# One decoder layer with 32 experts on one core: expert biases added by single fp32r matmuls, and expert weights read in runs of 16 KB

## What is computed

```python
t = rmsnorm(x, norm_moe).reshape(256, 1024)
top_v, top_i = lax.top_k(t @ w_router + b_router, 4)       # 4 of 32 experts for a token
combine = ...                                              # softmax of top_v, spread to (256, 32)
for w1, b1, w2, b2, ce in experts:                         # w1 (1024, 2048), w2 (1024, 1024)
    u = t @ w1 + b1
    g, lin = min(u[:, :1024], 7), clip(u[:, 1024:], -7, 7)
    y = (g * sigmoid(1.702 * g) * (lin + 1)) @ w2 + b2
    acc += ce[:, None] * y
```

## Time and profile before

| | |
|---|---|
| median of 3 runs | 1445.66 us (1444.25 to 1447.10) |
| profiled execution | 1445.8 us, the same as its span, first to last instruction |
| PE busy | 1379.8 us (95%) |
| DVE busy | 469.5 us (32%) |
| ACT busy | 343.7 us (24%) |
| HBM read | 473.0 MB |

### The profile page before, as it was taken

One profiled execution on the slowest core, in us unless ns is written; L12 is line 12 of the kernel. 1 busy time (PEld: TensorE's weight loads), 2 busy tenths in 40 slices (PEclk: granted clock), 3 DMA queues, 4 the chain that ended last, 5 costly groups with the idle time before them and its releaser, 6 DMA issues.

```text
span 1445.8 us, 18689 instructions
## 1 busy us (share of the span) xinstructions
PE 1379.8 (95%) x7799; PEld 758.1 (52%) x7799; DVE 469.5 (32%) x796; ACT 343.7 (24%) x494; POOL 10.2 (1%) x27
## 2 busy tenths in 40 slices
PE   6999999999998999999999999999999999999996
PEld 6999988999997333333333333333333333333332
DVE  4653554444565222212122122121221212212222
ACT  5454544564343110101101011010110101101102
POOL 1000000000000000000000000000000000000000
PEclk9999999999998899999999999999999999999998
DMA  9453533536459799999999999999899999999993
GB/s 297 150 191 127 175 121 126 221 117 251 175 207 369 289 409 410 409 410 410 410 410 410 410 410 410 409 410 410 344 411 410 410 410 410 410 410 410 409 410 141
DMA packets 141273, 474.68 MB, mean 328 GB/s; under 512 B 8112, under 2 KB 10224, under 8 KB 141200
## 3 DMA queue, kind: packets, MB, share of 16 engines
q1 hardware_dynamic: 139776, 473.01, 83.7%
q10 hardware_dynamic: 1456, 1.07, 0.3%
HBM read 473.02 MB, written 1.05 MB: 328 GB/s over the span
## 4 chain that ended last, share of the span: by engine, by line
PE 89%; DVE 6%; ACT 3%; issue 1%; DMA 0%; SPq 0%; DVEq 0%; ACTq 0%
PE bank L1330 52%; PE bank L1168 26%; PE bank L1398 4%; DVE big_a L1060 2%; DVE big_a L1064 2%; DVE big_a L1057 2%; PE bank L1383 1%; ACT fxqT L731 1%; ACT p_a L734 1%; PE bank L1331 1%; PE bank L1178 1%; DMA ring<-in_w_in 0%; PE bank L1270 0%; PE bank L1289 0%; PE bank L1246 0%
## 5 line engine op out<-in xcount | busy, mean ns | idle before, releaser
L1330 PE MATMUL bank<-place,fxqT 128*64 128x512 f32 x1536 | 678.0, 594 | 24.4 <-ACT fxqT L731 24.4
L1331 PE MATMUL bank<-place,fxqT 128*64 128x512 f32 x1536 | 678.2, 595 | 0.0
L1330 PEld LDWEIGHTS bank<-place,fxqT 128*64 128x64 f32 x1536 | 208.2, 137 | 452.0 <-issue 452.0
L1331 PEld LDWEIGHTS bank<-place,fxqT 128*64 128x64 f32 x1536 | 208.4, 137 | 0.0
L788 DVE TENSOR_TENSOR w_lo<-ring,w_hi 128x2048 fp32r<-128x2048 f32 x64 | 146.7, 2292 | 161.3 <-ACT w_hi L510 161.2
L510 ACT ACTIVATE w_hi<-ring 128x2048 fp32r<-128x2048 f32 x64 | 122.6, 1916 | 173.5 <-PE bank L1168 170.8
L1168 PE MATMUL bank<-h_hi,w_hi 128*128 128x256 f32 x448 | 130.1, 290 | 2.5 <-DVE h_lo L778 2.5
L1168 PE MATMUL bank<-h_lo,w_hi 128*128 128x256 f32 x448 | 128.4, 287 | 0.0
L1168 PE MATMUL bank<-h_hi,w_lo 128*128 128x256 f32 x448 | 128.3, 286 | 0.0
L1047 DVE TENSOR_TENSOR fxqT<-bank,cols 128x256 f32<-128x256 f32 x66 | 24.9, 419 | 265.3 <-PE bank L1343 265.3
L1057 DVE TENSOR_SCALAR big_a<-bank 128x512 f32<-128x512 f32 x32 | 22.1, 691 | 252.6 <-PE bank L1331 252.6
(11 more groups left out here) (255 smaller groups left out, 1737.6 us busy)
## 6 DMA issues: line engine op xcount, KB each, us to landing
place<-in_w_exp_in SPq DMA_DIRECT2D x128, 2048.0 KB, 19.2
place<-in_w_exp_out SPq DMA_DIRECT2D x64, 2048.0 KB, 15.1
ring<-in_w_in SPq DMA_DIRECT2D x19, 2048.0 KB, 7.8
ring<-in_w_branch SPq DMA_DIRECT2D x6, 2048.0 KB, 8.1
ring<-in_w_mem_kv SPq DMA_DIRECT2D x4, 2048.0 KB, 8.1
ring<-in_w_out SPq DMA_DIRECT2D x2, 2048.0 KB, 11.7
ring<-in_w_in SPq DMA_DIRECT2D x2, 1024.0 KB, 8.4
xs<-in_x SPq DMA_DIRECT2D x2, 512.0 KB, 4.2
```

The source lines that it names most:

```text
L1330: mm(o[0:CAP, :], lhsT, low, start=start, stop=stop)
L1331: return mm(o[CAP:P, :], lhsT, high, start=start, stop=stop)
```

## The change

1. A transfer of expert weights is laid out so that partition p holds four rows next to each other, 4p to 4p + 3 of its block of 512. For w2 that is one run of 16 KB. For w1, whose rows are 8 KB (gate and linear part), a transfer now takes two whole rows of each partition, again one run of 16 KB; a transfer then holds both parts, so PE goes over the four transfers with gate and linear part inside, and both accumulate until the fourth. The operands follow this order of rows: ScalarE writes `got` through a view that reads PSUM in steps of 4 floats, VectorE writes `act_out` in steps of 128 floats, and the gain comes from a new small tile `g_rows`.
2. The biases are split in a rounded part and what is left of it, both fp32r, stacked in four groups of 32 partitions (both column halves), and `pick_e` becomes a [128, 2, 64] fp32r operand that holds a one in four rows. One matmul with 128 output columns replaces a pair: two for b1 (at the start), one for b2.
3. To prepare that: four DMAs each for b1 and b2 on ScalarE's queue in place of one, b1's at slot 60 behind a wait for `o_split`, a rounding copy on ScalarE at slots 50 and 62 (each behind a wait for the DMAs), subtractions on GpSimd in place of the two clears, the table `row_of` on GpSimd, and `g_rows` by a DMA of 16-byte pieces at slot 0.
4. VectorE's gate step waits for `gate_done`, given after the last gate matmul of the fourth transfer, where it waited for the second transfer.

```diff
-                part_, low = j // 2, D // 2 * (j % 2)
-                src = w[:, low:low + D // 2, FF * part_:FF * (part_ + 1)].rearrange("e (k p) n -> p (e k) n", p=P)
-                sp.dma_start(w1_buf[p][j][:, :, :], src).then_inc(w1_in[p][j], 16)
+                half, q = j // 2, 2 * (j % 2)
+                src = w[:, D // 2 * half:D // 2 * (half + 1), :].rearrange("e (p q) n -> p (e q n)", q=4)
+                sp.dma_start(w1_buf[p][j][:, :, :].rearrange("p k n -> p (k n)"),
+                             src[:, 2 * FF * q:2 * FF * (q + 2)]).then_inc(w1_in[p][j], 16)
...
-                src = w[:, FF // 2 * j:FF // 2 * (j + 1), :].rearrange("e (k p) n -> p (e k) n", p=P)
+                src = w[:, FF // 2 * j:FF // 2 * (j + 1), :].rearrange("e (p q) n -> p (e q n)", q=4)
...
-            pool.memset(b2rows[:, :], 0.0).then_inc(b2_zero, 1)
...
-            pool.memset(b1rows, 0.0).then_inc(b1_zero, 1)
+            pool.memset(row_of[:, :, :], 0.0).then_inc(row_step, 1)
...
+            def what_is_left(raw, split, left):
+                for n, r in enumerate((32, 96)):
+                    pool.tensor_tensor(split[r:r + 32, :], raw[r:r + 32, :], split[r:r + 32, :].bitcast(F32),
+                                       ALU.subtract).then_inc(left, 1)
...
+                    act.dma_start(g_rows[:, :, :],
+                                  norm_moe[0].rearrange("(h p q) -> p h q", h=2, q=4)).then_inc(router_in, 16)
...
+                if i == 50:
+                    act.wait_ge(b2_in, 64)
+                    act.activation(b2split[:, :], b2raw[:, :], ACT.Copy).then_inc(b2_rounded, 1)
+                if i == 60:
+                    act.wait_ge(o_split, 6)
+                    for r in range(4):
+                        half = b_exp_in[0].rearrange("e (q h n) -> e q h n", q=2, h=2)[:, :, r // 2, :]
+                        act.dma_start(b1raw[32 * r:32 * r + 32, :].rearrange("e (q n) -> e q n", q=2),
+                                      half).then_inc(b1_in, 16)
                 if i == 62:
-                    act.wait_ge(b1_zero, 1)
-                    act.dma_start(b1rows[0:NE, :], b_exp_in[0]).then_inc(b1_in, 16)
+                    act.wait_ge(b1_in, 64)
+                    act.activation(b1split[:, :], b1raw[:, :], ACT.Copy).then_inc(b1_rounded, 1)
...
-                act.activation(got, bank[2][:, :], ACT.Copy).then_inc(got_ready, 1)
+                act.activation(got.rearrange("c (q p) -> c q p", q=4), bank[2][:, :].rearrange("c (p q) -> c q p", q=4),
+                               ACT.Copy).then_inc(got_ready, 1)
...
-                dve.wait_ge(w1_used[p][1], mg + 1)
+                dve.wait_ge(gate_done, n + 1)
...
-                dve.tensor_tensor(act_out, lin, sig, ALU.mult).then_inc(act_ready, 1)
+                dve.tensor_tensor(act_out.rearrange("c (q p) -> c p q", q=4), lin.rearrange("c (p q) -> c p q", q=4),
+                                  sig.rearrange("c (p q) -> c p q", q=4), ALU.mult).then_inc(act_ready, 1)
...
                 for part_ in range(2):
-                    o, c = bank[part_], FF * part_
-                    both_halves(o, pick_e[:, :], b1rows[:, c:c + 512], b1rows[:, c + 512:c + FF], True, False)
...
+                    mm(bank[part_][:, :], pick_all, b1split[:, 512 * part_:512 * (part_ + 1)], start=True, stop=False)
+                for j in range(W1):
+                    half = j // 2
+                    pe.wait_ge(w1_in[p][j], mg * 16 + 16)
+                    rows_ = w1_buf[p][j][:, :, :].rearrange("p (q a) n -> p q (a n)", q=2)
+                    for part_ in range(2):
+                        c = FF * part_
+                        for i in range(2):
+                            w = rows_[:, i, c:c + FF]
+                            ins = both_halves(bank[part_], gotT[:, 2 * (j % 2) + i, half, :], w[:, 0:512], w[:, 512:FF],
+                                              False, j == W1 - 1 and i == 1)
+                        if j == W1 - 1 and part_ == 0:
+                            ins.then_inc(gate_done, 1)
+                    ins.then_inc(w1_used[p][j], 1)
+                    if j == 1:
                         pe.wait_ge(put_added, n * 4 + 4)
-                        both_halves(bank[5], pick_e[:, :], b2rows[:, 0:512], b2rows[:, 512:D], True, False)
+                        mm(bank[5][:, :], pick_all, b2split[:, :], start=True, stop=False)
```

More of the change, by code:

```diff
@@ L144, in build @@
         gsig = big_a[:, 0:2 * D].rearrange("p (c s) -> p c s", c=KT)
-        merged = sb("merged", [P, KT, S])
-        qkT, kmT = merged, merged
-        b1rows = merged[:, :, :].rearrange("p c s -> p (c s)")
+        with nc.sbuf_tensor("merged", [P, KT, S], F32) as merged:
+            qkT, kmT = merged, merged
+        b1raw = sb("b1raw", [P, D])
+        b1split = sb("b1split", [P, D], F32R)
+        final_dump = big_a[:, 0:2 * D].rearrange("p (t d) -> p t d", t=TT)
         gfin = sb("gfin", [P, D])
@@ L165, in build @@
         wr = sb("wr", [P, KT, NE])
+        g_rows = sb("g_rows", [P, 2, 4])
         br = sb("br", [P, NE])
@@ L174, in build @@
         p_a = sb("p_a", [P, 512])
-        p_bt = sb("p_bt", [P, 1024])
-        p_b, p_t = p_bt[:, 0:512], p_bt[:, 512:1024]
-        b2rows = p_bt
+        with nc.sbuf_tensor("p_bt", [P, 1024], F32) as p_bt:
+            p_b, p_t = p_bt[:, 0:512], p_bt[:, 512:1024]
+        b2raw = sb("b2raw", [P, 512])
+        b2split = sb("b2split", [P, 512], F32R)
         negmax = sb("negmax", [P, 2])
@@ L198, in build @@
         yS = p_a[:, :]
-        pick_e = sb("pick_e", [P, CAP])
+        row_of = sb("row_of", [P, 2, NE + 1])
+        pick_e = sb("pick_e", [P, 2, CAP], F32R)
         sel = sb("sel", [P, TT, CAP])
@@ L293, in build @@
         sq_ready, rstd_ready = sem("sq_ready"), sem("rstd_ready")
-        b1_zero, b2_zero, round_end = sem("b1_zero"), sem("b2_zero"), sem("round_end")
+        round_end = sem("round_end")
+        row_step, row_of_ready = sem("row_step"), sem("row_of_ready")
+        b1_rounded, b1_left, b2_rounded, b2_left = (sem(n) for n in ("b1_rounded", "b1_left", "b2_rounded", "b2_left"))
         selT_done, selWT_ready = sem("selT_done"), sem("selWT_ready")
-        gate_ready, sig_ready, ffn_step, aT_ready = (sem(n) for n in ("gate_ready", "sig_ready", "ffn_step", "aT_ready"))
+        gate_done, gate_ready, sig_ready, ffn_step, aT_ready = (sem(n) for n in ("gate_done", "gate_ready", "sig_ready", "ffn_step", "aT_ready"))
         yS_ready, put_done, put_added = (sem(n) for n in ("yS_ready", "put_done", "put_added"))
@@ L460, in _ @@
                                        channel_multiplier=-1).then_inc(ml_masked, 1)
-            pool.wait_ge(proj_done, FIRST["g1"] + 1)
-            pool.memset(b2rows[:, :], 0.0).then_inc(b2_zero, 1)
-            pool.wait_ge(o_split, 6)
-            pool.memset(b1rows, 0.0).then_inc(b1_zero, 1)
+            pool.memset(row_of[:, :, :], 0.0).then_inc(row_step, 1)
+            pool.wait_ge(row_step, 1)
+            for half in range(2):
+                pool.affine_select(out=row_of[:, half, 0:NE], in_=row_of[:, half, 0:NE], compare_op=ALU.not_equal,
+                                   fill=1.0, base=-64 * half, pattern=[[-1, NE]],
+                                   channel_multiplier=1).then_inc(row_step, 1)
+            pool.wait_ge(row_step, 3)
+            for half in range(2):
+                pool.affine_select(out=row_of[:, half, 0:NE], in_=row_of[:, half, 0:NE], compare_op=ALU.not_equal,
+                                   fill=1.0, base=-64 * half - 32, pattern=[[-1, NE]],
+                                   channel_multiplier=1).then_inc(row_of_ready, 1)
+            def what_is_left(raw, split, left):
+                for n, r in enumerate((32, 96)):
+                    pool.tensor_tensor(split[r:r + 32, :], raw[r:r + 32, :], split[r:r + 32, :].bitcast(F32),
+                                       ALU.subtract).then_inc(left, 1)
+                    pool.wait_ge(left, n + 1)
+            pool.wait_ge(row_of_ready, 2)
+            pool.wait_ge(b2_rounded, 1)
+            what_is_left(b2raw, b2split, b2_left)
+            pool.wait_ge(b1_rounded, 1)
+            what_is_left(b1raw, b1split, b1_left)
         ALL_CONSTS = 9
@@ L1039, in pick_expert @@
             def pick_expert(e):
-                dve.tensor_copy(pick_e[:, :], ident[:, bass.ds(e, 1)].to_broadcast([P, CAP])).then_inc(pick_ready, 1)
+                dve.tensor_copy(pick_e[:, :, :],
+                                row_of[:, :, bass.ds(e, 1)].to_broadcast([P, 2, CAP])).then_inc(pick_ready, 1)
             def take_turned(k):
                 dve.wait_ge(got_turned, k)
-                weights = g_moe.rearrange("p (h q) -> p q h", h=2)
+                weights = g_rows[:, :, :].rearrange("p h q -> p q h")
                 for h in range(2):
@@ L1094, in experts @@
                 dve.sem_inc(round_end, 1)
+            dve.wait_ge(row_of_ready, 2)
             dve.sem_inc(put_added, 4)
```

(5 more changed lines are left out.)

22 lines of the change are left out of this document (7 added, 15 removed).

## The result

| | before | changed |
|---|---|---|
| median | 1445.1 us (1444.3 to 1447.1, 4 runs) | 1415.1 us (1412.8 to 1415.8, 4 runs) |
| ratio | | 0.9784 (95%: 0.9770 to 0.9798) |
| profiled execution: span, time | 1445.8, 1445.8 us | 1411.0, 1412.8 us |
| TensorE's period, an expert | 29.98 us | 29.01 us |
| read rate in the expert stage | 410 GB/s | 428 GB/s |

The kernel became 2.2% faster. The forecast was 1403 us; the measured time lies 12 us above it, inside the range of 1388 to 1430.

The account below looks back on a forecast made before the run. TensorE was taken to set the pace with DMA close behind. 1445.8 us less 42.9 (32 experts at 28.64 us each), less 0.4 for the first expert's clock, plus 0.5 for preparation gave 1403.0 us; range 1388 to 1430.

Parts of the forecast that it names:

- windows of 410 to 420 GB/s, set by PE: Sign expected in the expert stage: read rate of 410 to 420 GB/s, with TensorE setting it.
- runs of 16 KB: Expert weight loads: 2 MB in 4.85 us in place of 5.115, from a fixed 11.8 ns a run.
- B: Expert loads: long runs gain less than the two rates say, 1406 us at half the step, 1419 at a quarter; chance 0.11.
- C: Expert loads: long runs do nothing, 410 GB/s stays and DMA binds, span 1432 us; chance 0.11.
- D: Expert loads: DMA gets worse as engines collide in memory, slower than before from 5.19 us a load; chance 0.04.
- the strided write: VectorE's act_out step in each expert, written in jumps of 512 bytes: 0.36 us more, bounds 0 and 0.7.
- Rival A: Expert stage: strides cost nothing, 28.28 us an expert, 1391.5 us; inside the forecast's range, which had chance 0.66.
- That `got` costs nothing: ScalarE's read of PSUM in steps of 16 bytes: no cost to TensorE even at double length, at most 0.2 us.
- the changes of array shape: The b2 matmul between pairs of 64 columns: going to the full array and back adds 0.15 us an expert.
- nothing is added there: Expert's start: L1398 was taken as full-array beside the full-array b1 matmul, so no shape cost, 0 us.
- E: New bias matmuls at 0.43 us and shape changes at 0.4: 0.82 us more an expert, 1429 us; chance 0.07.
- the hole at the change of order: Read gap where w2(19) waits for TensorE to leave w2(18): shrinks from 4.3 us to 1.3 us.

Follow-up runs that it names:

- The bias half alone: Changed kernel with weights back in four runs of 4 KB and got and act_out in order, split biases kept: 1438.5 us, ratio 0.9946 against the kernel before.
- The 8 KB experiment: Changed kernel with each w1 transfer in two runs of 8 KB a partition, w2 still at 16 KB: 1416.0 us, ratio 0.9780 against the kernel before.

## Why the prediction was right or wrong

**Right: what bounds.** TensorE sets the pace before and after, and DMA stands close behind. The bias half alone shows it best: without quicker loads it gives 8 us. One sign I gave was wrong by my own sum: I expected windows of 410 to 420 GB/s, set by PE. At 29.1 us of loads an expert against a period of 28.64, loads are always queued and the window shows DMA's own rate, as it did (428).

**Right: runs of 16 KB.** 428 GB/s, where two rates gave 434 and I took 432. A 2 MB load takes 2097152 / 428e3 = 4.90 us and a run (eight to an engine) 612.5 ns, so with the 159.8 ns of 4 KB the fixed part is (4 x 159.8 - 612.5) / 3 = 8.9 ns a run, not 11.8. The 8 KB experiment agrees with this size. By it runs of 2 KB would go at 389 GB/s; the window of the earlier trace rows that had 382 held other work too, which may be why, and no run shows it. Rivals B, C and D fall. The Trainium skill (DMA: Bandwidth & Descriptors, "Why small descriptors are slow") would have had 417 GB/s; the measurement decides.

**Right: the strided write.** 0.36 us was taken from a reduction read in jumps, 1.05 - 0.69 = 0.36 was measured. Rival A falls. That the two agree so closely is luck: the one is a read in jumps of 128 bytes, the other a write in jumps of 512. That `got` costs nothing held too, but for a better reason than mine: it does not get longer at all.

**Wrong in size: the changes of array shape.** The step "That is 0.15 us; bounds 0 and 0.4", and "nothing is added there" for b1. Against 0.24 a matmul plus 0.15, b2 measured 0.57 (0.18 more) and the two b1 0.67 (0.19 more). Together 0.37 us an expert: 28.64 + 0.37 = 29.01, the whole error of the period, 11.8 us in 32 experts. The price of the way back, 0.05, came from 705.18 in the earlier trace rows, where TensorE had just waited 0.76 us for ScalarE, so that whatever else it costs lay in the wait. Between busy matmuls a visit to the full array costs 0.2 more; the runs show this price once a visit, and not how the way in and the way back share it. The Trainium skill (TensorEngine Tiling (Array Packing), "Key Properties") says that changing the tiling mode drains TensorE; it has no figure, and the runs show what it costs here: 0.2 us a visit between busy matmuls and, as far as can be seen, none of it in a wait. At the expert's start I had taken L1398 for a full-array matmul with nothing added behind it. Its matmuls use 64 rows, a shape of their own, and leaving it costs the same towards either shape. Before, then in the changed kernel, the last four records of L1398 and what follows:

```profile
713.99 1.05 PE L1398 MATMUL bank<-p_a,fxqT 64*128 64x512 f32 x4
714.97 0.64 PE L1330 MATMUL bank<-merged,pick_e 128*64 128x512 f32 x1
```

```profile
703.06 1.05 PE L1446 MATMUL bank<-p_a,fxqT 64*128 64x512 f32 x4
704.05 0.51 PE L1403 MATMUL bank<-b1split,pick_e 128*128 128x512 f32 x1
```

0.98 and 0.99 us. So leaving the 64 rows costs what it did, the visit to the full array behind it is new, and I had left it out.

**Which rival this is.** The chance was highest for 1388 to 1410, and the time missed that. It lies where B had put it (1406 to 1420), but by luck: B's cause, slower loads, did not come. It is half of E, for which I had worked out 1416: of its two parts the fp32r matmuls cost no more than forecast and the changes of shape 0.37 us. I had given E 0.07.

**From the forecast to the measured time.** 1403.0 + 11.8 = 1414.8, against 1415.1 for the median. The profiled execution is 2.4 below its median. Its first expert started at full granted clock (half clock, 1.2 GHz, ended at 469 us, before it ended at 478), against 0.68 in the earlier trace rows:

```profile
470.00:482.00 12.00, 10.68 (x49) 3.88 (x51) 0.99 (x4) 1.70 (x2) 0.00 (x0) 1.00 0.43 165
```

Its mean granted clock is 0.989, that of the other three executions 0.986; that these ran at half clock for longer at this place is likely but not shown: the profiled execution of the kernel before has 0.989 too, with half clock up to 478. From the first bias record to the end of w2 of the last expert the two traces differ by 33.7 us: 32 x 0.975 = 31.2, and 2.6 for the 5.1 us that before ran at half clock.

**Wrong, without effect: the hole at the change of order.** I had 1.3 us, on the idea that a smaller lead shrinks it. Windows of the changed kernel over the hole, after it and at the end of the loads, and SyncE's queue:

```profile
1008.00:1018.00 10.00, 8.72 (x44) 3.04 (x42) 3.67 (x9) 2.10 (x4) 0.00 (x0) 1.00 0.00 0
1050.00:1380.00 330.00, 313.51 (x1423) 109.20 (x1424) 82.98 (x171) 37.44 (x62) 0.00 (x0) 1.00 1.01 428
...
1380.00:1385.00 5.00, 5.00 (x26) 1.60 (x24) 0.23 (x1) 0.00 (x0) 0.00 (x0) 1.00 0.23 95
```

```profile
1017.04 0.34 SPq L351 DMA_DIRECT2D place<-in_w_exp_out  x1
```

Nothing is read for 10 us. The issue of w2(19), which waits for TensorE, came at 1017.04 and 21.7 us earlier than the 1038.69 of the earlier trace rows; the loads queued ahead of it were done by about 1007, where it had been 1035 before (178 GB/s over 1034 to 1036, 4 over the next 2 us). So the hole grew because DMA gained more than TensorE. With it the loads ended at about 1381 (95 GB/s over 1380 to 1385) and not at 1365.8: by DMA alone the span would be 1381 + 4.8 + 14.1 = 1400, still below the 1411 that TensorE set, so the hole cost nothing. The 1.3 us were worked out for the case in which DMA binds and then used in the other.

**Nearly wrong: ScalarE's wait for b1.** I expected b1 to have landed at 445. Line L739, its four loads, and then ScalarE's timeline:

```profile
DMA to landing us min/median/max: 8.0/11.5/13.4
```

```profile
451.54 1.06 ACT L743 ACTIVATE b1split<-b1raw 128x1024 fp32r<-128x1024 f32 x1 [6.15 <-DMA b1raw<-in_b_exp_in]
...
454.92 0.42 ACT L690 ACTIVATE big_c<-xs 128x256 f32<-128x256 f32 x1 [1.52 <-DVE xs L847]
```

The four loads took 8.0 to 13.4 us in place of 6.5, beside transfers of 16 KB runs, and 1.5 us of the 9 us of cover were left. The sum of squares on the path started at 454.92, 0.3 us later than in the earlier trace rows; the preparation cost 0.3 us, 0.5 was taken. Whether the length of the runs next to them made b1's loads slow was argued beforehand and not tried by itself: there are also four in place of one.

## What to carry to other kernels

Price an instruction that changes the shape of TensorE's array from a place where the engine is busy on both sides, and put such instructions next to others of the same shape, best in a wait. When two resources run within a few per cent of each other, work out what each would give alone: a saving on one is paid out only as far as the other lets it, and halves of a change can be worth less than nothing by themselves. A reordered layout costs where a step on the path writes or reads it in jumps; the same reordering can be given to an engine for which it is cheap.

## What the runs showed of the hardware

- Between busy matmuls, a change from pairs of 64 columns to the full array and back costs about 0.33 us beyond the matmul itself (b2: 0.57 - 0.24), whether one matmul stands there or several. About 0.1 of it shows ahead of the first full-array matmul, the rest behind it. A change between float32 and fp32r on the full array costs nothing that the starts show.
- An fp32r matmul of 128x512 costs 0.22 to 0.25 us in a row of them; the trace gives it 0.39 to 0.50 us.
- VectorE writes 512 floats in jumps of 512 bytes in 1.05 us against 0.69 in order. ScalarE reads PSUM in steps of 16 bytes at no cost (0.60 us both ways), and TensorE's four transposes of an operand in steps of 16 bytes take 0.08 us more.
- HBM to SBUF from one core: 410 GB/s in runs of 4 KB, 424 with w1 in runs of 8 KB, 428 in runs of 16 KB.
- GpSimd's subtraction of 32x1024 floats takes 2.4 us, of 32x512 2.1 us (means of two each; the spans of this engine are rough).
